# An unnormed first product with its scale at the evictions, and state space tables built by rows

## The reference

```python
def rms_norm(x, g):
    return x * rsqrt(mean(x * x, axis=-1) + EPS) * g

def layer_ab(x, norm_g, w_in, ...):
    h = rms_norm(x, norm_g)
    g_q, g_k, g_v, g_lr, g_gate, f_q, f_k, f_v, f_f, f_gate = split(h @ w_in)
    log_a = log_sigmoid(g_lr @ alpha_up + alpha_b) / GLA_TAU
    o = gla_chunked(g_q, g_k, g_v, log_a)          # gated linear attention
    ...
# the layer behind it holds a state space part (S5): groups of 16 channels share
# a 64-dim complex diagonal state, x_t = Lbar x_{t-1} + Bbar u_t, y_t = Re(C x_t) + D u_t
```

## Time and profile before

| | before |
|---|---|
| median of 3 runs | 3431.4 us (3431.08 to 3432.77) |
| the profiled execution | 3432.28 us |
| its span | 3430.5 us |
| granted TensorE clock, mean | 0.991 |
| PE busy | 3341.5 us (97%) |
| DVE busy | 1638.5 us (48%) |
| ACT busy | 1291.4 us (38%) |
| DMA | 525.06 MB, mean 153 GB/s |

### The profile page before, as it was taken

One profiled execution on the slowest core, in us unless ns is written; L12 is line 12 of the kernel. 1 busy time (PEld: TensorE's weight loads), 2 busy tenths in 40 slices (PEclk: granted clock), 3 DMA queues, 4 the chain that ended last, 5 costly groups with the idle time before them and its releaser, 6 DMA issues.

```text
span 3430.5 us, 41764 instructions
## 1 busy us (share of the span) xinstructions
PE 3341.5 (97%) x16431; PEld 2700.0 (79%) x16431; DVE 1638.5 (48%) x2695; ACT 1291.4 (38%) x2000; POOL 515.0 (15%) x749
## 2 busy tenths in 40 slices
PE   7999999999999999999999899999999999999998
PEld 6777887887888888888888676788878888777886
DVE  7895655344343454444343556553424343355443
ACT  4443433343233333433342436532323323355432
POOL 0001312322110000110330011021000111110211
PEclk9999999999999999999999999999999999999999
DMA  6776433546348776544335343363433643433642
GB/s 211 216 231 199 132 105 105 154 145 208 132 160 227 210 215 184 173 159 141 123 111 170 119 129 102 122 214 119 147 88 111 200 151 117 132 111 102 208 148 92
DMA packets 279523, 525.06 MB, mean 153 GB/s; under 512 B 64189, under 2 KB 99588, under 8 KB 274720
## 3 DMA queue, kind: packets, MB, share of 16 engines
q1 hardware_dynamic: 223504, 340.79, 33.0%
q0 software_dynamic: 53648, 178.32, 15.2%
q10 hardware_dynamic: 2176, 3.28, 0.4%
HBM read 408.32 MB, written 113.97 MB: 152 GB/s over the span
## 4 chain that ended last, share of the span: by engine, by line
PE 73%; DVE 3%; ACT 3%; issue 2%; DMA 1%; POOL 0%; ACTq 0%; POOLq 0%; DVEq 0%
PE pg L631 64%; PE pm L1322 2%; PE pm L1351 2%; PE pm L1338 1%; PE pm L2426 1%; ACT whi L390 1%; DMA mx_g<-zt 1%; PE pm L2430 0%; PE pm L2414 0%; DVE r_y L1707 0%; DVE d_x L2514 0%; PE pm L2405 0%; ACT stage L501 0%; PE pm L1819 0%; ACT w_p L1387 0%
## 5 line engine op out<-in xcount | busy, mean ns | idle before, releaser
L396 DVE TENSOR_TENSOR wlo<-raw,whi 128x1024 fp32r<-128x1024 f32 x523 | 663.2, 1273 | 1251.5 <-ACT whi L390 1250.5
L390 ACT ACTIVATE whi<-raw 128x1024 fp32r<-128x1024 f32 x523 | 548.7, 1054 | 1100.3 <-PE pg L631 1090.2
L631 PE MATMUL pg<-a_hi,whi 128*128 128x512 f32 x1856 | 743.9, 401 | 11.4 <-DVE wlo L396 4.8
L631 PE MATMUL pg<-a_hi,wlo 128*128 128x512 f32 x1856 | 726.7, 392 | 0.0
L631 PE MATMUL pg<-a_lo,whi 128*128 128x512 f32 x1856 | 726.2, 391 | 0.0
L631 PE MATMUL pg<-b_hi,whi 128*128 128x512 f32 x1568 | 620.8, 396 | 8.7 <-DVE stage L572 3.2
L631 PE MATMUL pg<-b_hi,wlo 128*128 128x512 f32 x1568 | 612.2, 390 | 0.0
L631 PE MATMUL pg<-b_lo,whi 128*128 128x512 f32 x1568 | 611.5, 390 | 0.0
L631 PEld LDWEIGHTS pg<-a_hi,whi 128*128 128x128 f32 x1856 | 348.4, 188 | 90.7 <-issue 14.2
L631 PEld LDWEIGHTS pg<-a_hi,wlo 128*128 128x128 f32 x1856 | 348.1, 188 | 77.5
L631 PEld LDWEIGHTS pg<-a_lo,whi 128*128 128x128 f32 x1856 | 348.7, 188 | 73.6 <-issue 2.6
(11 more groups left out here) (442 smaller groups left out, 3843.7 us busy)
## 6 DMA issues: line engine op xcount, KB each, us to landing
raw<-in_l_w_in SPq DMA_DIRECT2D x169, 512.0 KB, 3.7
raw<-in_ab_w_in SPq DMA_DIRECT2D x112, 512.0 KB, 3.7
zt<-stage POOLq DMA_DIRECT2D x142, 256.0 KB, 3.6
raw<-in_c_w_in SPq DMA_DIRECT2D x64, 512.0 KB, 4.9
raw<-in_l_w_out SPq DMA_DIRECT2D x64, 512.0 KB, 3.9
raw<-in_ab_w_out SPq DMA_DIRECT2D x32, 512.0 KB, 3.8
raw<-in_glu_w SPq DMA_DIRECT2D x32, 512.0 KB, 4.2
raw<-in_c_w_out SPq DMA_DIRECT2D x32, 512.0 KB, 3.7
```

Of the source, the lines that this page charges most:

```text
L390: nc.scalar.activation(used(whi, n), used(raw, n), ACT.Copy).then_inc(hi_ready, 1)
L396: nc.vector.tensor_tensor(used(wlo, n), used(raw, n), used(whi, n).bitcast(F32), ALU.subtract).then_inc(lo_ready, 1)
L631: ins = nc.tensor.matmul(pg[m][:r.rows(m), :r.cols()], lhsT, rhs, start=(kt == 0 and n_pass == 0), stop=(kt == r.kts - 1 and n_pass == 2))
```

## The change

It has two parts. **The first norm.** x comes in four blocks of columns, so that whole tiles of the transposed x are there early. The first weight pieces are issued ahead of nearly all parameters. PE transposes tiles 0 to 3 before the first product and two more in each of the units 1 to 6 of the first block. The operands are made of g times x, without `rstd`. The sums over tokens are made in units 7 to 11, the parameters in units 8 to 12, and every bank of GLA_IN, FOX_IN and AB_GATES is multiplied by `rstd` when it is evicted: 41 banks whose tokens lie along the free axis by a DVE tensor operation (before by ACT alone), the others by ACT with a scale. **The tables.** `s_B` is transposed (2 transposes a slice) and stored to DRAM as rows; the powers are stored once. 24 loads a slice repeat these rows over 8 groups of 16 partitions (`repeat_rows`), 2.1 MB a slice, and `b_powers` of slice `sl - 1` is made in slot `sl`, in the layout that is stored, from `s_Br` and `s_Pr`. The lead of the phase goes from 4 to 7 pieces.

```diff
 def turn_in_pool(pool):
+            if n == 2:
+                pool.wait_ge(raw_in[2], 16)
+            pool.dma_start(XT["x_tok"][:, :, columns], inp["x"][0, :, columns].rearrange("(t p) d -> p t d", p=P)).then_inc(tokens_moved[n], 16)
...
 def first_block_pe(pe, unit):
+        for kt in front_tiles(unit):
+            turn_x_pe(pe, kt)
...
 def operand_hi(act, kt):
+        nc.scalar.activation(A["a_hi"][:, kt, :], XB["xb"][:, kt, :], ACT.Copy, scale=col("ab_norm_g", kt)).then_inc(nh_ready, 1)
 def operand_lo(dve, kt):
+        nc.vector.scalar_tensor_tensor(out=A["a_lo"][:, kt, :], in0=XB["xb"][:, kt, :], scalar=col("ab_norm_g", kt),
+                                       in1=A["a_hi"][:, kt, :].bitcast(F32), op0=ALU.mult, op1=ALU.subtract).then_inc(h_ready, 1)
...
-    SCALED = {n: C_U0 for n in (C_U0, C_REST)}
+    SCALED = {n: GLA_IN for n in (GLA_IN, FOX_IN, AB_GATES)}
+    SCALED.update({n: C_U0 for n in (C_U0, C_REST)})
...
 prep_sp
+        def repeat_rows(sl):
+            for e in range(ST):
+                rows_of = slice(e * SC, (e + 1) * SC)
+                power = powers_rows[:, e:e + 1, sl * SPAIR:(sl + 1) * SPAIR, :].rearrange("n a j x -> a n (j x)")
+                sp.dma_start(V5["s_Pr"][rows_of, :, :, :].rearrange("p n j x -> p n (j x)"),
+                             power.broadcast_to([SC, 2, SPAIR * P])).then_inc(rows_repeated, 16)
+                for n in range(2):
+                    sp.dma_start(V5["s_Br"][rows_of, n, :, :], b_rows[sl][:, n, :].rearrange("(j c) x -> c j x", c=SC)).then_inc(
+                        rows_repeated, 16)
...
+            if at == 3 and 0 < sl <= SSL:
+                sp.wait_ge(s5_l, 2 * sl)
+                sp.dma_start(bt_dram[sl - 1], V5["s_BT"][:, :, :, :].rearrange("p n j x -> p (n j x)")).then_inc(b_tables_kept, 16)
+            if at == 3 and 0 <= sl < SSL:
+                sp.wait_ge(s5_bte, sl + 2)
+                sp.dma_start(b_rows[sl], V5["s_bT"][:, :, :]).then_inc(rows_kept, 16)
+            if at == 4 and 0 <= sl < SSL:
+                sp.wait_ge(rows_kept, 16 * (sl + 2))
+                repeat_rows(sl)
             if at == 5 and 0 <= sl < SSL:
-                sp.wait_ge(s5_bte, 2 * sl + 2)
-                keep(bt_dram, V5["s_BT"][:, :, :, :].rearrange("p n j x -> p (n j x)"), sl)
...
 b_powers(sl, n)
+            if n == 0:
+                dve.wait_ge(rows_repeated, 16 * ROW_LOADS * (sl + 1))
+                dve.wait_ge(rows_kept, 16)
+                dve.wait_ge(b_tables_kept, 16 * sl)
+            to, by, tp = V5["s_BT"][:, n, :, :], V5["s_Pr"], t.rearrange("p j e c -> p j (e c)")
+            run(tt(to, V5["s_Br"][:, n, :, :], by[:, 0, :, :], ALU.mult))
...
+            if at in (1, 2) and 0 < sl <= SSL:
+                b_powers(sl - 1, at - 1)
...
-        beside(prep_pe(pe), PREP_STEPS, pe, pe_piece, GLA_IN, 4)
+        beside(prep_pe(pe), PREP_STEPS, pe, pe_piece, GLA_IN, 7)
```

More of the change, by code:

```diff
@@ L478, in act_piece @@
             split_hi(act, r.piece0 + i * r.pieces + q + AHEAD)
+        if r is PHASES[GLA_IN][1][0] and i == 0:
+            first_block_act(act, 2 * q + part)
+        if part == 0:
             return
@@ L551, in dve_piece @@
             split_lo(dve, r.piece0 + i * r.pieces + q + AHEAD)
+        if r is PHASES[GLA_IN][1][0] and i == 0:
+            first_block_dve(dve, 2 * q + part)
+        if part == 0:
             return
@@ L608, in pe_piece @@
             token_rows_pe(pe, MT * (i - 1) + q - 2)
+        if r is PHASES[GLA_IN][1][0] and i == 0:
+            first_block_pe(pe, 2 * q + part)
         if joint is not None and r is extra["first"] and i == 0 and part == 0:
@@ L767, in turn_in_pool, with x_landed, front_tiles, turn_x_pe @@
+    def x_landed(eng, kt):
+        for n, (k0, k1) in enumerate(X_BLOCKS):
+            if k0 <= kt < k1:
+                eng.wait_ge(tokens_moved[n], 16)
+    def front_tiles(unit):
+        return range(2 * unit + 2, 2 * unit + 4) if 0 < unit <= LAST_FRONT_UNIT else ()
+    def turn_x_pe(pe, kt):
+        x_landed(pe, kt)
+        if kt >= 4:
+            pe.wait_ge(xt_ev, kt - 3)
         for t in range(NTOK):
-            pool.dma_start(XT["x_tok"][:, t, :], inp["x"][0, t * P:(t + 1) * P, :]).then_inc(tokens_moved[t], 16)
+            ins = nc.tensor.transpose(pm[kt % 4][:, t * P:(t + 1) * P], XT["x_tok"][:, t, kt * P:(kt + 1) * P], ident[:, :])
+        ins.then_inc(xt_ready, 1)
@@ L792, in turn_in_pe @@
[L792 to L796, removed]
+        pe.wait_ge(ident_in, 32)
+        nc.tensor.transpose(pg[3][:, :KT], rows[:KT, 0, :], ident[:KT, :KT]).then_inc(cols_turned, 1)
+        for kt in range(MT):
+            turn_x_pe(pe, kt)
+        pe.wait_ge(cols_ready, 1)
@@ new lines, in first_block_pe @@
+    def first_block_pe(pe, unit):
+        for kt in front_tiles(unit):
+            turn_x_pe(pe, kt)
+        if unit == 10:
+            pe.wait_ge(s5_th, 1)
+            pe.wait_ge(xt_ev, 13)
+            for i in range(3):
+                ins = nc.tensor.transpose(pm[0][:, i * NPAIR:(i + 1) * NPAIR], s5_natural(i), ident[:NPAIR, :NPAIR])
+            ins.then_inc(s5_ct, 1)
+        if unit == 12:
+            pe.wait_ge(consts_in, 16 * NCONST)
+            pe.wait_ge(xt_ev, KT)
+            for r in range(2):
+                w = min(NROWS - r * P, P)
+                ins = nc.tensor.transpose(pm[1][:, r * P:r * P + w], rows[:w, r, :], ident[:w, :w])
+            ins.then_inc(cols_turned, 1)
+            pe.wait_ge(sd_ready, 1)
+            for t in range(NTOK):
+                ins = nc.tensor.matmul(pm[2][:, t * P:(t + 1) * P], rstd_col[:, t:t + 1].broadcast_to([P, P]), ident[:, :], start=True, stop=True)
+            ins.then_inc(rs_ready, 1)
@@ L809, in turn_in_act @@
[L809 to L813, removed]
-    def turn_in_dve(dve):
+        split_hi(act, 0)
+        act.wait_ge(cols_ready, 1)
+        for kt in range(MT):
+            operand_hi(act, kt)
+        split_hi(act, 1)
@@ new lines, in turn_in_dve @@
+    def turn_in_dve(dve):
+        dve.wait_ge(cols_turned, 1)
+        nc.vector.tensor_copy(cols[:, :KT], pg[3][:, :KT]).then_inc(cols_ready, 1)
+        dve.wait_ge(cols_ready, 1)
+        for kt in range(2):
+            dve.wait_ge(xt_ready, kt + 1)
+            nc.vector.tensor_copy(XB["xb"][:, kt, :], pm[kt][:, :]).then_inc(xt_ev, 1)
+        split_lo(dve, 0)
+        for kt in range(2):
+            operand_lo(dve, kt)
+        tiles_dve(dve, range(2, MT))
+        split_lo(dve, 1)
+        split_lo(dve, 2)
@@ L816, in turn_in_dve, with first_block_dve @@
+    def first_block_dve(dve, unit):
         run = serial(dve, dve_seq)
```

274 lines of the change are left out of this document (138 added, 136 removed).

## The result

The changed kernel takes 3546.22 us in the median (3542.31 to 3551.96, 4 runs), the kernel before 3431.24: a ratio of 1.0337 (1.0321 to 1.0354). The direction was forecast, the size was not: 3499 (3445 to 3538) was expected, 68 us more, and 115 came.

The account below looks back on a forecast made before the run. PE, 97% busy, bounds the kernel, DVE second; the change's serial row loop delays the gate matmul by 63.8 us. With +2.4 for half clock and +1.4 for evictions, +67.6 on 3432.3: 3500, as median 3499 (3445 to 3538).

Parts of the forecast that it names:

- The end of the phase: From the last `b_powers` at 363.2 to the gate matmul at 389.2, before at 325.36: +63.8 us.
- the size of the turn: Tables' loop, one `b_powers` to the next: 33.0 us, 5.3 more in four of seven; 252.2 in all, 36.0 each.
- The row of 141 GB/s: Profile row of `d_MG`'s loads into 16 partitions, taken as the repeated rows' rate: 2.1 MB a slice in 14.9 us.
- the rival of the slower rows: Tables' row loads slower by 5.3 us a turn, if 16 partitions at a time bear less: 3536 us, chance 0.11.
- The first turn: First `b_powers` of the tables, slice 0's, was to start at 111, near where slice 1's stood before.
- Where PE would wait: Some 19 us of PE's waiting at the linear attention's gate matmul, the rest in products for `wlo`.
- PE would reach the linear attention 31 us earlier: If nothing else held: start -14.7 us and PE's work in the tables -16.5.
- the first product: Start of the kernel: PE's first product at 13.7 us (12 to 15), before at 28.39.
- the block's end: End of the first block at 67.7 us, before at 82.4: -14.7.
- the rival "faster": Tables' rows land in time and DVE bounds a slot, +10.2 us there; -19.6 in sum, 3412, chance 0.13.
- a gain of 16.5 from transposes: PE's work in the tables: 16 runs of 8 transposes and waits go, 19.8 us; 3.3 come in: -16.5.
- the rival at 3412: Tables' rows and landing need 12 us together, not 21, so DVE bounds a slot: 3412 us, chance 0.13.

Follow-up runs that it names:

- tables_alone: The kernel before with only the changed tables' functions (24 row loads a slice), old start and lead of 4 pieces: 3544.4 us, ratio 1.0325.
- few_bytes: The changed kernel with its 24 row loads a slice bringing an eighth of the bytes from slice 1 on: 3493.5 us, one run.
- rows_pool: The changed kernel with its 24 row loads a slice issued by POOL instead of SP, rows of B stored a step earlier: 3501.7 us, ratio 1.0203.
- norm_alone: The changed kernel with the tables' functions of the kernel before, so only the first norm's part, lead of 7 pieces kept: 3429.7 us, ratio 0.9999.
- norm_less: norm_alone with DVE's product into `s_tp` (two a slice) left out from slice 1 on: 3417.8 us, ratio 0.9959.
- norm_act: norm_alone, whole computation, with the phases' first product and two fills moved from DVE to ACT, 1.18 us a slot: 3423.0 us, ratio 0.9971.
- before_less: The kernel before with DVE's product into `s_tp` left out from slice 1 on: 3430.2 us, ratio 0.9997.
- norm_lead5: norm_alone with sums and parameters three units earlier in the first block and a lead of 5 pieces: 3432.7 us, ratio 1.0002.
- norm_pool: norm_alone with the product into `s_tp` made by POOL a step ahead, into two buffers: 3452.6 us, ratio 1.0060.
- narrow_4k: The changed kernel, still 24 loads a slice into 16 partitions each, with all rows read in 4 KB pieces: 3531.4 us, one run.
- wide_rows: The changed kernel with a slice's 2.1 MB of rows in 4 loads into 128 partitions each, 4 KB pieces: 3537.4 us, ratio 1.0305.

## Why the prediction was wrong

**The mechanism held.** The forecast took the serial turn of rows, `b_powers`, store and landing as the bound, and it is (tables_alone, few_bytes, rows_pool). The end of the phase was sized to 0.1 us, 26.0 forecast from the last `b_powers` to the gate matmul and 25.9 measured (412.23 to 438.09), with some luck: 13.4 to the `s_bt` store (13.9 forecast), 5.6 to POOL's first load (6.9) and 6.9 from there (5.2) cancel out.

**The failed step is the size of the turn**: "The turn: 0.47 + 0.45 + 6.4 + 1.3 + 14.9 + 0.8 + 7.5 + 1.13 = 33.0", with 5.3 in four of seven. The mean was 36.0 forecast, 41.6 measured; seven times 5.6 are 39 us of the miss. By its three parts, means of the seven turns:

| us | forecast | measured |
|---|---|---|
| from `b_powers` to the `s_bt` store | 7.5 + 1.13 + 5.3 in four of seven: 11.7 | 15.0 |
| to the first row load | 0.47 + 0.45 + 6.4 + 1.3: 8.6 | 4.8 |
| the rows, to `b_powers` | 14.9 + 0.8: 15.7 | 21.8 |

The rows are the term that was mis-sized most. The row of 141 GB/s was too fast for them: 108 to 116 GB/s moved while they were issued, and 2.1 MB in 21.8 us are 96. No run or row shows the 5.3 us a turn, 37 in all, by which the rival of the slower rows lies above 3499; the rows took 6.1 a turn more than forecast in its place (21.8 for 15.7). The way to the `s_bt` store was taken as `b_powers` and, in four turns, the `s_k` stores with a piece. But the `s_k` stores stand there in all seven turns, and the next slice's input loads, 6.6 us of issues in the turn shown, in six of them, wholly or in part; the prediction has them in no turn. Against both stands the middle part: the stored rows don't seem to queue behind the store of 1 MB (they landed after 4.2 us in the median, 4.4 at most, where 6.4 was taken), and the piece, where one stands there, is issued while SP waits for their landing, which hides the 1.3 added for it. "Nothing landed there below 5" holds for the `s_bt` stores before (5.6 at least), but not for the queue. Of its stores of 32 KB in the earlier trace rows's stretch the view says:

```profile
s_k<-s_K SPq DMA_DIRECT2D x56, 32.0 KB, 2.9
```

**The first turn**: 111 forecast for the first `b_powers`, 121.3 measured, 10 us more. DVE was ready at 109.1 (12.21 idle), as forecast, but the first rows, issued from 99.35, needed their 22 us too. That first wait was left out of the sum. 39 + 10 are the 49 us by which the gate matmul missed (389.2 forecast, 438.1).

**Where PE would wait** was wrong as well. The prediction had 19 us at the gate matmul and the rest in products for `wlo`. PE waited 4.4 us at the gate, 2.5 for `wlo` and 94.3 at the transposes of `s_cn`, for inputs that stand behind the rows and the late piece in SP's queue.

**"If nothing else held, PE would reach the linear attention 31 us earlier"** was wrong too, hidden by the loop. norm_alone has 14 us of it at the first product (14.24) and 18 at the block's end, and gives them all back. Its window from 90 to 280 us, then those of norm_less and of the kernel before:

```profile
90.00:280.00 190.00, 173.68 (x1006) 140.20 (x1005) 175.41 (x204) 76.88 (x131) 11.06 (x19) 0.98 0.72 224
```

```profile
90.00:280.00 190.00, 180.69 (x1052) 146.52 (x1052) 168.37 (x202) 81.21 (x137) 11.04 (x19) 1.00 0.74 237
```

```profile
90.00:280.00 190.00, 184.97 (x1065) 147.59 (x1064) 168.12 (x194) 81.97 (x141) 12.79 (x20) 1.00 0.73 227
```

PE's busy time falls from 185.0 to 173.7 in these 190 us, 11 us more of waiting. 8.7 of it are waits for `s_L` (14.4 us in norm_alone, 5.7 before, 9.4 in norm_less, 10.1 in norm_act). DVE's busy time rises from 168.1 to 175.4, with ten operations more; ten evictions with the scale at 0.683 would be 6.8. Waits of PE in norm_alone and norm_act:

```profile
PE pm L2182 <- DVE s_L L2357: 14.4, 9, 2.8
```

```profile
PE pm L2182 <- DVE s_L L2371: 10.1, 8, 2.8
```

The prediction called DVE the second bound with a microsecond of room, and let it eat 10.2 us in the rival "faster" alone, beside a gain of 16.5 from transposes. That DVE's load takes most of the start's gain, 12.4 of 18 us, is shown by norm_less and before_less; the rest isn't explained, and the later beginning of the steps isn't ruled out by norm_lead5. By these the rival at 3412 looks too low; no run here had both fast rows and the freed transposes, so that stays open.

**Right** were the first product, the block's end within 4 us, the nearly missing waits at the tables' transposes (3.3 us in all), DVE's wait for the rows before `b_powers` (12.2 to 17.6 us a slice, where 8 to 12 were forecast), and the DMA share over 1.

## What to carry to other kernels

A chain through DRAM is sized by everything in the issuing queue between its steps: list that queue in order for one turn, with each wait, and count all of it. Time won ahead of a phase that a second engine nearly fills can be lost again, as here; test it by leaving out one of that engine's operations in both versions. Here DVE got more room when ACT took some of its work (3423.0 us, norm_act), and became slower when POOL took a product of two tensors (two operations of 0.29 us took 2.23; 3452.6, norm_pool); the operations moved weren't the same ones.

## What the runs showed of the hardware

Two DVE operations of 0.29 us took 2.23 each beside a 128x1152 product on POOL (norm_pool). 2.1 MB in 24 loads into 16 partitions each took 20.0 us in 4 KB pieces (narrow_4k) and 21.8 with 512 B pieces for half of it, with other traffic beside them; while they were issued 108 to 116 GB/s moved. With the same 2.1 MB in 4 loads of 512 KB into 128 partitions each the DMA share fell to 0.51, at 153 GB/s, with bytes still to move (wide_rows). With the same 24 loads issued by POOL's queue (median 0.53 us each, SP 0.43) and the rows' store a step earlier the kernel took 44.6 us less, with DMA engines at a share of 1.00. In two turns of the change a pair of input loads took over 8 us to issue (from 160.61 and from 287.77), right behind 5 MB of rows, stores and pieces; why wasn't tested.
